# Window keys loaded by position class, masks and first gate weights loaded during the prompt attention, gate products placed at the change from keys to values

## The reference

```
proj = h @ w_in -> q_A k_A v_A q_B k_B v_B, forget logits, gate_A, gate_B
A: 12 heads, windows (128, 512, 2048) with dilations (1, 4, 16); B: 8 heads, all past rows
prompt: o_A, o_B over the prompt's own rows
sample: o_A over window buffers, o_B over the paged cache
mix = (sigmoid(gate_A) * (o_A @ w_pa) + sigmoid(gate_B) * (o_B @ w_pb)) @ w_o
x = x + gate1 * RMSNorm(mix); then a mixture of 32 experts
```

## Time and profile before

| | |
|---|---|
| three timed runs | 1197.62, 1197.81, 1199.43 us; median 1197.81 |
| the profiled execution | 1199.27 us, of which the traced span is 1197.5 us |
| busy of the span | PE 84%, DVE 32%, ACT 17%, POOL 16% |
| mean granted TensorE clock | 0.914 of full speed |
| `phase_b` ends, `phase_c` starts | 395.0 us |
| `phase_c` ends, `phase_d` starts | 794.4 us |

### The profile page before, as it was taken

The page is one execution under the profiler, slowest core; times in us unless marked ns, Lnnn a source line. Parts: engine busy times, 40 slices in busy tenths (PEclk is TensorE's granted clock), DMA queues, the critical chain, the costliest instruction groups (busy, mean ns, idle before and its releaser), DMA issues. The chain is left out here.

```text
span 1197.5 us, 17987 instructions
## 1 busy us (share of the span) xinstructions
PE 1000.1 (84%) x7324; PEld 585.3 (49%) x7324; DVE 379.9 (32%) x865; ACT 206.0 (17%) x509; POOL 187.3 (16%) x210
## 2 busy tenths in 40 slices
PE   3999999997897169979989997579977998777770
PEld 2444444444564046647656674136554554444430
DVE  3100033237751164516701771003451222100105
ACT  3000000014542011100020003001231211111114
POOL 0000033311200100022222311100003322212110
PEclk9999999999997589989989998669978999989995
DMA  9976666977787779998969984979187999999966
GB/s 339 355 278 248 249 248 248 326 244 255 256 212 168 207 240 213 289 349 322 370 231 334 364 320 151 391 266 341 57 325 269 364 370 383 379 393 394 397 256 237
DMA packets 98062, 348.48 MB, mean 291 GB/s; under 512 B 13018, under 2 KB 56802, under 8 KB 78654
## 3 DMA queue, kind: packets, MB, share of 16 engines
q1 hardware_dynamic: 80478, 265.90, 64.8%
q0 software_dynamic: 15552, 79.97, 18.1%
q10 hardware_dynamic: 1952, 1.48, 0.5%
HBM read 335.46 MB, written 63.36 MB: 333 GB/s over the span
## 5 line engine op out<-in xcount | busy, mean ns | idle before, releaser
L1605 PE MATMUL bank<-turned,w_all 128*128 128x320 f32 (+1 forms) x512 | 143.7, 425 | 0.0
L442 PE MATMUL bank<-w_all,turned 128*128 128x481 f32 (+2 forms) x384 | 119.3, 503 | 1.1 <-DVE turned L651 1.1
L442 PE MATMUL bank<-w_ring,turned 128*128 128x481 f32 (+2 forms) x384 | 118.4, 502 | 0.0
L2013 PE MATMUL bank<-w_all,mix_row 128*64 128x256 f32 x736 | 92.2, 407 | 26.9 <-DMA w_all<-in_w_exp 25.8
L1605 PEld LDWEIGHTS bank<-turned,w_all 128*128 128x128 f32 x512 | 95.3, 196 | 35.6 <-issue 15.5
L2013 PEld LDWEIGHTS bank<-w_all,mix_row 128*64 128x64 f32 x736 | 60.9, 147 | 65.3 <-issue 46.4
L1709 DVE STREAM_TRANSPOSE mods<-w_all 128x2048 f32<-128x2048 f32 (+1 forms) x39 | 86.6, 2239 | 9.8 <-PE bank L1481 7.1
L442 PEld LDWEIGHTS bank<-w_all,turned 128*128 128x128 f32 (+1 forms) x384 | 56.8, 171 | 61.5 <-issue 58.3
L442 PEld LDWEIGHTS bank<-w_ring,turned 128*128 128x128 f32 (+1 forms) x384 | 57.1, 171 | 60.4 <-issue 57.3
L2059 DVE COPY act_t<-bank 128x128 f32<-128x128 f32 x33 | 9.6, 292 | 200.8 <-PE bank L2023 199.1
L661 DVE COPY w_all<-bank 128x481 f32 (+5 forms) x32 | 16.9, 531 | 152.6 <-PE bank L442 152.4
(11 more groups left out here) (357 smaller groups left out, 1318.5 us busy)
## 6 DMA issues: line engine op xcount, KB each, us to landing
w_all<-in_w_exp SPq DMA_DIRECT2D x22, 2048.0 KB, 41.0
out_a_sample<-in_cache_a SPq DMA_DIRECT2D x8, 4080.0 KB, 21.4
w_all<-in_w_exp SPq DMA_DIRECT2D x25, 1024.0 KB, 39.2
mods<-in_w_ada SPq DMA_DIRECT2D x21, 1024.0 KB, 8.8
w_all<-in_cache_a SPq DMA_DIRECT2D x96, 128.0 KB, 7.5
w_all<-in_cache_a SPq DMA_DIRECT2D x40, 256.0 KB, 6.1
turned<-in_w_exp SPq DMA_DIRECT2D x5, 2048.0 KB, 42.2
mods<-in_w_exp SPq DMA_DIRECT2D x5, 2048.0 KB, 43.7
```

Of the source, the lines that this page charges most:

```text
L442: mm = nc.tensor.matmul(m.banks[i][r:r + ROWS[i], 0:hi - lo], m.hT[:, k, i * P:i * P + ROWS[i]], ring[u][:, CW * k + lo:CW * k + hi], star ...
L1605: mm = nc.tensor.matmul(GATE[:, 0:WIDTH[h]], gate_w[b][k][:, c % 2 * P:(c % 2 + 1) * P], m.hT[:, k, 256 * h:256 * h + WIDTH[h]], start=k = ...
L2013: mm = nc.tensor.matmul(m.banks[2 + p][x * SLOTS:(x + 1) * SLOTS, 0:HID], hgT[:, k, :], m.weights(u)[:, (2 * k + x) * HID:(2 * k + x + 1) ...
```

## The change

1. `window_keys_in`: one transfer per pair (x, c) to all 128 partitions, in place of one per pair (j, x) to 32 partitions. The number, the sizes (128 KB) and the rows of 1 KB stay. The source, which had a group of 32 positions outermost, now has the 4 sequences outermost, then 32 positions.
2. The window mask (now one transfer of 0.85 MB), the gate weights of the first pair (2 MB) and its merge weights (0.75 MB) are requested inside `phase_b`'s list: mask and first half after piece 13, the second half after piece 14, the merge weights after piece 15. Before the first gate weights SP waits for the last `turn` of `phase_b`. They lie in six slices a tile instead of seven.
3. DVE waits for the mask only at the first `add_bias`, for the constants at the last of an "a" unit, and works out page rows at step 7.
4. Of the 80 pieces, 2 come right after the last key step of each unit (`late_at`) and 5 right before its first value step; the other 52 go evenly over the remaining steps up to 87. ACT does the tanh of late pieces before `exps`, and for "b" units one between the two.

```diff
 def window_keys_in(eng, I, slot, arrived, u, g):
     name, t, t0 = window_of(g)
     n = min(t, 2)
-    for j in range(4):
-        src = I[name][4 * u + j].rearrange("(c i t) n -> i t c n", c=4, t=t)[:, t0:t0 + n, :, 0:AH * HD]
-        dst = slot[32 * j:32 * j + 32, 0:n * 4 * AH * HD].rearrange("p (t c n) -> p t c n", t=n, c=4)
-        for x in range(n):
-            eng.dma_start(dst[:, x], src[:, x]).then_inc(arrived, 16)
+    src = I[name][4 * u:4 * u + 4].rearrange("s (c i t) n -> s i t c n", c=4, t=t)[:, :, t0:t0 + n, :, 0:AH * HD]
+    for x in range(n):
+        for c in range(4):
+            dst = slot[:, (4 * x + c) * AH * HD:(4 * x + c + 1) * AH * HD]
+            eng.dma_start(dst, src[:, :, x, c]).then_inc(arrived, 16)
+
+
+def gate_weights_in(eng, I, m, p, b):
+    src = I["w_gates"][2 * b + p // 2].rearrange("p (k n) -> p k n", k=KD)[:, :, (p % 2) * 256:(p % 2 + 1) * 256]
+    for lo, hi in ((0, 6), (6, 8)) if b == 0 else ((0, 4), (4, 8)):
+        at = (8 * b + lo) % 6
+        dst = m.low[(8 * b + lo) // 6][:, at * 256:(at + hi - lo) * 256]
+        eng.dma_start(dst.rearrange("p (k n) -> p k n", n=256), src[:, lo:hi, :]).then_inc(m.gate_in[b], 16)
+
+
+def merge_weights_in(eng, I, m, p):
+    cols = slice(256 * p, 256 * (p + 1))
+    for name, lo, hi in (("w_pa", 16, 18), ("w_pb", 18, 22)):
+        dst = m.low[lo // 6][:, lo % 6 * 256:(lo % 6 + hi - lo) * 256].rearrange("p (k n) -> p k n", n=256)
+        eng.dma_start(dst, I[name].rearrange("p (k n) -> p k n", n=D)[:, :, cols]).then_inc(m.merge_in, 16)
@@ phase_b, SyncE
             for k in range(1, KV_RING - 1):
                 early_keys(k)
                 piece(BEFORE + 1 + k)
+                if k == 2:
+                    sp.dma_start(m.wmask, I["mask_window"]).then_inc(m.mask_in, 16)
+                    sp.wait_ge(turn_a, len(turns))
+                    sp.wait_ge(turn_d, len(turns))
+                    gate_weights_in(sp, I, m, 0, 0)
+                if k == 3:
+                    gate_weights_in(sp, I, m, 0, 1)
+            merge_weights_in(sp, I, m, 0)
@@ phase_c
-    FIRST, END = 3, 80
-    piece_at = {}
-    for n, x in enumerate(pieces):
-        piece_at.setdefault(FIRST + n * (END - FIRST) // len(pieces), []).append(x)
-    step_of = {x: t for t, xs in piece_at.items() for x in xs}
+    LATE, TURN, END = 2, 5, 88
+    first_v = [at[(u, "v", 0)] for u in range(len(UNITS))]
+    rate = (len(pieces) - len(UNITS) * (LATE + TURN)) / (END - 1 - len(UNITS))
+    piece_at, late_at, todo, due = {}, {}, list(pieces), 0.0
+    for t in range(1, N):
+        due += 0 if t in first_v else rate
+        count = TURN if t in first_v else min(int(due + 1e-6), len(todo))
+        due -= 0 if t in first_v else count
+        piece_at[t], todo = todo[:count], todo[count:]
+        if t + 1 in first_v:
+            late_at[t], todo = todo[:LATE], todo[LATE:]
@@ phase_c, SyncE
             window(KV_RING - 1)
-            gate_weights(0, 0)
-            for j in range(4):
-                sp.dma_start(wmask[32 * j:32 * j + 32, :], I["mask_window"]).then_inc(con_in, 16)
             sp.dma_start(consts[:], I["sample_consts"]).then_inc(con_in, 16)
-            gate_weights(0, 1)
-            merge_weights(0)
@@ phase_c, VectorE
+                    dve.wait_ge(m.mask_in, 16)
+                    if c == 3:
+                        dve.wait_ge(con_in, 16)
...
+            def rows_of_pages():
+                dve.wait_ge(pages_in, 16 * 2)
...
             turn(0)
-            dve.wait_ge(pages_in, 16 * 2)
...
-            dve.wait_ge(con_in, 16 * 5)
...
+                    if (u, part, g) == (0, "v", 0):
+                        rows_of_pages()
...
+                for x in late_at.get(t, []):
+                    if x[0] == "out":
+                        mixing(*x[1:3])
```

More of the change, by code:

```diff
@@ L129, in build @@
         m.wp_in, m.wo_in = [ctx.enter_context(nc.semaphore(n)) for n in ("w_p", "w_o")]
+        m.gate_in = [ctx.enter_context(nc.semaphore(f"gate_w{b}")) for b in range(2)]
+        m.merge_in, m.mask_in = [ctx.enter_context(nc.semaphore(n)) for n in ("merge_w", "mask_rows")]
         with ExitStack() as attn:
@@ L214, in constants @@
             "over_ids": np.arange(EXPERTS, BLOCKS, dtype=np.float32)[None, :],
-            "mask_window": np.concatenate(window, axis=1), "sample_consts": sample_consts,
+            "mask_window": np.tile(np.concatenate(window, axis=1), (4, 1)), "sample_consts": sample_consts,
             "page_consts": np.concatenate([before, seq_of, tri8], axis=1),
@@ L1232, in phase_c @@
             pieces += [("gate", c, h, 1, 0), ("gate", c, h, 1, 4), ("out", c, h, 0, 0)]
-    FIRST, END = 3, 80
-    piece_at = {}
-    for n, x in enumerate(pieces):
-        piece_at.setdefault(FIRST + n * (END - FIRST) // len(pieces), []).append(x)
-    step_of = {x: t for t, xs in piece_at.items() for x in xs}
+    LATE, TURN, END = 2, 5, 88
[9 more added lines that the diff above has]
+            late_at[t], todo = todo[:LATE], todo[LATE:]
+    assert not todo
+    step_of = {x: t for xs in (piece_at, late_at) for t, ys in xs.items() for x in ys}
+    LAST_PIECE = max(step_of.values())
     items = [x[1:3] for x in pieces if x[0] == "out"]
@@ L1269, in phase_c @@
         sc_b = m.sc.rearrange("p (h n) -> p h n", h=2)
-        slices = [m.low[i][:, 256 * x:256 * (x + 1)] for i in range(4) for x in range(7)]
+        slices = [m.low[i][:, 256 * x:256 * (x + 1)] for i in range(4) for x in range(6)]
         gate_w = [slices[0:8], slices[8:16]]
         wp_a, wp_b = slices[16:18], slices[18:22]
-        th_a = {x: slices[22 + x] for x in range(4)}
-        th_b = slices[26:28]
+        th_a = {x: m.low[x][:, 1536:1792] for x in range(4)}
+        th_b = slices[22:24]
         flat_wa = m.wa[:].rearrange("p u f q -> p (u f q)")
@@ L1296, in phase_c @@
         bias_in = [sem(f"bias{x}") for x in range(4)]
-        gate_in, wp_in = [sem(f"gate_w{b}") for b in range(2)], sem("merge_w")
+        gate_in, wp_in = m.gate_in, m.merge_in
         gain_in, terms, terms_out = sem("gains"), sem("terms"), sem("terms_out")
@@ L1339, in gate_weights @@
             def gate_weights(p, b):
[L1340 to L1345, removed]
-            def merge_weights(p):
[L1348 to L1355, removed]
+                sp.wait_ge(gate_pe, sum_of[(2 * p - 1, 1, b)] + 1)
+                gate_weights_in(sp, I, m, p, b)
+            def merge_weights(p):
+                sp.wait_ge(out_pe, 4 * p)
+                merge_weights_in(sp, I, m, p)
             def past_bias(u, x):
@@ L1617, in _ @@
                     (score if STEPS[t][1] == "k" else weigh)(t)
+                for x in late_at.get(t, []):
+                    piece(*x)
                 for x in use_at.get((t, "after"), []):
@@ L1656, in gates, with exps @@
                 ins.then_inc(th_ok, 1)
-            def exps(u):
+            def exps(u, between):
                 for h in range(1 if kind(u) == "a" else 2):
+                    if h:
+                        for x in between:
+                            gates(*x)
                     e = u if kind(u) == "a" else 2 + 2 * own(u) + h
@@ L1666, in _ @@
             for t in range(N + 1):
-                for x in piece_at.get(t, []):
-                    if x in sums:
-                        gates(*x)
+                now = [x for x in piece_at.get(t, []) if x in sums]
+                for x in now[1:] if t in first_v and kind(STEPS[t][0]) == "b" else now:
+                    gates(*x)
                 for x in use_at.get((t, "before"), []):
@@ L1687, in _ @@
                 if t + 1 < N and STEPS[t][1] == "k" and STEPS[t + 1][1] == "v":
-                    exps(STEPS[t][0])
-                if t == max(piece_at) + 2:
+                    for x in late_at[t]:
+                        if x in sums:
+                            gates(*x)
+                    exps(STEPS[t][0], [x for x in piece_at[t + 1] if x in sums][:1])
+                if t == LAST_PIECE + 2:
                     act.wait_ge(mixed, 2 * KD)
@@ L1826, in _ @@
             use_dve = {"shares": shares, "fold": out_cols, "totals": past_sums}
-            turn(0)
-            dve.wait_ge(pages_in, 16 * 2)
[L1829 to L1833, removed]
-            dve.wait_ge(con_in, 16 * 5)
+            def rows_of_pages():
+                dve.wait_ge(pages_in, 16 * 2)
+                for j in range(4):
+                    rows = slice(32 * j, 32 * j + 32)
+                    for dst, ids in ((key_rows, page_ids[rows].rearrange("p (u s g) -> p u s g", u=2, s=4)[:, :, j, :]),
+                                     (value_rows, page_ids[rows].rearrange("p (s x g) -> p s x g", s=NSEQ, x=4)[:, :, :, j])):
+                        V.tensor_scalar(dst[rows].rearrange("p (a b) -> p a b", a=ids.shape[1]), ids, 32.0, run_id[rows, 0:1], ALU.mult, ALU.add).then_inc(idx_ok, 1)
+            turn(0)
             for t in range(N + 1):
```

5 lines of the change are left out of this document (3 added, 2 removed).

## The result

The changed kernel takes 1263.3 us (median of 4 runs, 1260.2 to 1265.0) against 1198.6 us for the kernel before beside it (1197.6 to 1203.2): a ratio of 1.0529, 95% interval 1.0493 to 1.0565. Slower, as forecast, and in the range; but 65 us slower where the sum said 39.

A forecast was written before the change was run, and what follows sets the result against it. TensorE is busy nearly everywhere but for a hole at 395 to 427 us. Paged keys +49 and paged units -10 sum to +39 on 1199.3, so 1238 us; range 1203 to 1290.

The forecast's parts named there:

- Four shares: Key transfers: four outermost sequences put each on four of sixteen DMA engines, 11.3 us a key step; chance 0.70.
- The first rival: Key transfers: all sixteen engines at the values' rate, faster, about 1159 us; chance 0.15.
- `phase_b`: Last `w_ada` piece used 24 us later, from four slow key steps and the moved masks and gates.
- The part of the moves: In `phase_b`'s queue, moved transfers cost 10 us of DMA time, 8.4 of it ahead of `w_ada` piece 15.
- from 343.3 us: Start of the `phase_b` sum: four key steps 45.2, four `w_ada` pieces 12, masks and gates 8.4; landing near 409.
- Unit a0: Head of `phase_c`: first weighing at 460 against 449.9, +10, the removed wait having given back 14.
- Change to values of a1 and its values: After unit a1's last keys: change 18 us instead of 5.7, value stage shrinking to 25 us.
- The paged units: Last two units of `phase_c`: together 242 us in place of 252, a gain of 10, bounds 0 to 20.
- the stages behind them are no longer at the DMA's limit: Paged units: loading nothing during the pieces at a change adds nothing to the sums; key stages 49 us.
- The third rival: Four shares, but long groups hurt too: paged units lose 10 instead of gaining, 1258 us; chance 0.12.
- my bound of 13.5 us a tile: Key tiles: upper price, for rows of 1 KB with all four streams to the same ports, giving 1265 us.
- The signs: Profile after: key rate near 90 to 100 GB/s, DMA share near 0.25, landings lost, waits moved, paged units shorter by some 10.

The follow-up runs named there:

- old keys: The changed kernel with the key transfers put back to their old form, all else still changed: 1183.5 us, ratio 0.990 to the kernel before.
- moves only: The kernel before with only the moved masks, first weights and deferred VectorE waits; old key transfers, pieces placed evenly: 1180.0 us, ratio 0.982.
- new keys alone: The kernel before with only the new key transfers: 1273.7 us, ratio 1.062.
- merged rows: The changed kernel with position classes reordered so that sequence and position merge into 128 outermost source rows in the key transfers: 1170.3 us, ratio 0.976.
- the placement alone: The kernel before with only the new placement of the pieces: 1197.5 us, ratio 1.000.
- groups of 3 pieces: The changed kernel with 128 merged source rows for keys, 1 late piece and 2 ahead of the first values at each change: 1156.8 us, ratio 0.968.
- 8 outermost: The changed kernel with key transfers of one sequence each, rows taken so that 8 are outermost and can't be merged: 1195.6 us, ratio 1.000.

## Why the prediction was right in kind and short in size

**The key transfers: right, and they are the whole loss.** Four shares were forecast from the missing landing of an 8-row transfer and the values' rate divided by four, 11.3 us a step; 11.3 to 11.7 were measured. Undone, the change is faster than before. The first rival (sixteen engines, 1159 us) was worked for a form that the change doesn't have; where the form was given sixteen shares it measured 1170.3.

**`phase_b`: +24 forecast, +35.2 at the last `w_ada` piece, +37.5 at the phase's end. This is the term that was most mis-sized, by 13.5 us.** The part of the moves held: 8.4 forecast, 9.2 and 9.4 measured from the first key request on (old keys, moves only). The part of the keys did not: the sum without the moved transfers gives 401.5 us at piece 15, 15.8 more than before, and new keys alone measured 22.7. Two steps of the sum failed.

The first is its start, "from 343.3 us": I took the queue up to there as unchanged, and the key request went out at 349.1. Of these 5.8 us, 3.6 stand already in the first key request (327.5 in place of 323.9), ahead of anything that was changed; merged rows has the same 327.5. The other 2.2 are the change's: `early_keys(0)` is a key tile as well, and its issue holds SyncE 10.1 us. In the kernel after the next key request follows it by 21.5 us, in the kernel before by 19.4 and with merged rows too:

```profile
327.54 4.30 SPq L255 DMA_DIRECT2D w_all<-in_cache_a  x8
...
346.90 3.66 SPq L255 DMA_DIRECT2D w_all<-in_cache_a  x8
```

So I counted four slow tiles where there are five, but the fifth costs 2 us and not 11. The second is the price of a key tile with its `w_ada` piece, 14.3 us. From 349.1 the rest of the sum (65.6 us to the landing, 1 of latency) gives 415.7, and 420.9 was measured, 5 us over. With new keys only the same sum without the moves gives 407.3 against 412.7, again 5 over: four pairs at about 15.6 us each. So it lies in these pairs and not in the moved transfers; why a pair takes 1.3 us more stays open.

**Unit a0: -14 forecast for the removed wait less the slow tiles, -5.1 measured.** The wait behind the page table is gone and the group took what it should (last key at 460.8, first weighing 21.4 us later; 22 were summed). The miss lies in step 5's tile: requested at 433.0, its issue holds SyncE 9.1 us and it is turned at 451.9, 18.9 us where I had 11.3. The sum took the transfer to start with its request and to have its engines to itself; GpSimd requests bias tables at 434.9 to 438.7 us beside it. How the 7.6 us split was not separated. In unit a1 the sum held: first weighing to last key 91 us, 88 summed.

**Change to values of a1 and its values: 43 us summed, 40.7 measured.** Right.

**The paged units: -10 forecast, -3.9 measured, -4.7 with the placement alone.** The stages one by one: first keys 46.7 us (49 summed), change 18.0 (18), first values 46.5 (47), second keys 59.0 (49), change 18.2 (18), last stage 59.8 (61). One step failed: "the stages behind them are no longer at the DMA's limit". The key stages stand at shares of 1.02 and 0.97 and at 391 and 357 GB/s, in place of 0.94 and 345, 0.90 and 329. The sum also had nothing loaded during the pieces at a change. That is so in the second paged group only; two stretches of the kernel after, one in each group:

```profile
664.00:676.00 12.00, 10.76 (x46) 8.12 (x45) 1.70 (x6) 3.76 (x7) 0.00 (x0) 1.00 0.96 361
790.00:802.00 12.00, 11.46 (x52) 9.21 (x52) 1.18 (x3) 5.68 (x9) 0.00 (x0) 1.00 0.00 0
```

And this idle group stands behind the slow key stage, not ahead of it; the value stage that follows it took 59.8 us, less than summed. So a debt left by a group does not explain the 59.0 us. The rows show this much: the second key stage moves 21.1 MB (59.0 us at 357 GB/s), the first 18.3 (46.7 at 391); among it are the next pair's gate and merge weights, requested at 741.1 to 746.9 us. A small transfer issued behind them is then late, in the timeline after:

```profile
753.11 12.07 SPq L1392 DMA_DIRECT2D bias<-c_past  x2
...
768.62 0.69 DVE L1741 CUSTOM_DVE_ANT_0 w_all<-bank,bias 128x512 f32<-128x512 f32 x1 [6.74 <-DMA bias<-c_past]
```

Its issue holds SyncE 12.1 us, DVE stands 6.7 us for this bias of the past, and TensorE behind it. That is part of the 10 us that the stage ran over; with groups of 3 pieces the same weights are requested in the stage as well, and it came to 47.4 us, so the rest stays open. The third rival (groups cost the paged units 10) is refuted in that form: DVE's waits for out pieces are 3.7 us in that stage, and the units did gain, by 4. How much of this gain is the placement's is not settled either: 4.7 us with it alone, none between moves only and old keys.

**The likeliest case, and the others.** Four shares as summed held in mechanism; its size lay at my bound of 13.5 us a tile (1265), though for another reason: in unit a1 the tile cost what I had taken. The miss of 27 us between the two profiled executions is 13.5 in `phase_b`, 9 in unit a0, 3 in unit a1 and 6 in the paged units, less 4 in the rest.

**The signs.** The rate, the share, the missing landing, the removed wait, some 18 us of pieces at each change and the waits for turns in steps 14 to 20 (46 us summed over the seven rows above) came as written. The waits for `w_ada` pieces 14 and 15 were 18.1 us, not over 20, and the paged units shortened by 4, not 10. And the sag of TensorE that the prediction puts at slices 25 and 26 is in slices 26 and 27 of the earlier trace rows; the times beside it are right.

## What to carry to other kernels

Before a transfer is reshaped to reach more partitions, look at its source's outermost dimension: with 4 or 8 entries there that could not be merged it ran at the rate of four or eight shares, and what stood behind it in a strict queue waited. Reordering which rows form a class, so that two dimensions merge, gave three and a half times the rate for one strided write on TensorE. Follow a slower transfer through all of its uses from the first request on, since its issue holds the queue too. And work gathered at one place is not free because the sum of the work is the same: here groups of seven pieces shortened the paged units by 7 us against none and lengthened the window units by 16, which only a split by unit shows.

## What was not expected of the hardware

- The issue itself takes longer with few shares: the 8 transfers of the first key tile hold SyncE 10.1 us in the kernel after (four outermost), 5.3 with 8 outermost, 4.2 to 4.3 before and with merged rows. Later tiles of `phase_b` take longer in both forms: up to 13.9 us after, up to 9.6 before.
- An old key tile to 32 partitions shows a share of 1.15 at only 210 GB/s; with 8 shares 190 GB/s cost a share of 0.55. So nearly the same rate can be had with half of the engines' busy time, and a share near 1 says nothing about the rate.
- TensorE starved for keys runs at a granted clock of 0.50 (the lower of its two levels, 1.2 GHz) even while it is busy 7.9 of 9 us, in 385 to 394 us of the kernel after; ahead of it, from 378 to 385 us, it had been busy 2.0 of 7 us. Its busy time over the whole span is 1012.0 us after and 1000.1 before, for the same work; how much of these 12 us is on the path was not separated.
